# A delta-rule recurrence: whole 128x128 transposes in place of 64x64 products, one kind of work at a time

## The reference

```
def step(state, inp):
    r_t, w_t, k_t, v_t, an_t, b_t = inp
    sa = jnp.einsum('bhij,bhj->bhi', state, an_t)
    state = (state * w_t[:, :, None, :] + sa[..., None] * b_t[:, :, None, :]
             + v_t[..., None] * k_t[:, :, None, :])
    return state, jnp.einsum('bhij,bhj->bhi', state, r_t)
```

## Time and profile before

| | us |
|---|---|
| median of 3 runs | 4853.73 |
| lowest and highest | 4845.61 to 4868.58 |
| span of the profiled execution | 4860.3 |
| TensorE matmul busy in it | 4200.5 |
| VectorE, ScalarE, GpSimd busy | 2967.3, 2069.0, 1175.3 |

### The profile page before, as it was taken

The page is one execution under the profiler, slowest core; times in us unless marked ns, Lnnn a source line. Parts: engine busy times, 40 slices in busy tenths (PEclk is TensorE's granted clock), DMA queues, the critical chain, the costliest instruction groups (busy, mean ns, idle before and its releaser), DMA issues. The chain is left out here.

```text
span 4860.3 us, 142503 instructions
## 1 busy us (share of the span) xinstructions
PE 4200.5 (86%) x61166; PEld 3925.7 (81%) x61166; DVE 2967.3 (61%) x5380; ACT 2069.0 (43%) x3696; POOL 1175.3 (24%) x952
## 2 busy tenths in 40 slices
PE   6979999976999967777777769972999999999998
PEld 5869999966888857667667757762999999999998
DVE  6879999945888854444444437757444444444443
ACT  4568888844666621111111112220444444444443
POOL 4544444421444410100011113310111211112110
PEclk9989999967999988999998989985999999999999
DMA  8810000014443331122111226630655655656553
GB/s 168 185 53 23 25 25 23 24 33 146 146 143 133 124 124 56 56 59 66 56 56 56 64 73 180 200 110 28 177 170 172 181 169 178 176 175 173 175 175 104
DMA packets 519591, 542.01 MB, mean 112 GB/s; under 512 B 75200, under 2 KB 456384, under 8 KB 519104
## 3 DMA queue, kind: packets, MB, share of 16 engines
q1 hardware_dynamic: 411840, 425.00, 27.8%
q10 hardware_dynamic: 92480, 62.93, 5.5%
q0 software_dynamic: 14784, 46.57, 4.6%
HBM read 377.99 MB, written 156.43 MB: 110 GB/s over the span
## 5 line engine op out<-in xcount | busy, mean ns | idle before, releaser
L2299 DVE TENSOR_TENSOR g_wlo<-g_raw,g_whi 128x2048 fp32r<-128x2048 f32 x192 | 439.2, 2287 | 115.5 <-ACT g_whi L2261 115.5
L2261 ACT ACTIVATE g_whi<-g_raw 128x2048 fp32r<-128x2048 f32 x192 | 366.4, 1909 | 145.2 <-DMA g_raw<-expert_w_gate 145.2
L2370 PE MATMUL g_pD<-g_whi,g_hh 128*128 128x256 f32 x1536 | 417.2, 285 | 2.5 <-ACT g_o L2288 2.4
L2370 PE MATMUL g_pD<-g_wlo,g_hh 128*128 128x256 f32 x1536 | 408.1, 279 | 0.0
L1119 PE MATMUL c_pP<-c_xh,c_whi 128*128 128x258 f32 x1120 | 329.8, 294 | 35.8 <-DMA c_gup<-g_lora_up 29.5
L1271 POOL TENSOR_TENSOR d_kr<-d_kr,d_fixed 128x512 f32<-128x512 f32 x80 | 104.8, 1316 | 1007.1 <-ACT d_kr L1305 1006.9
L1384 DVE TENSOR_TENSOR d_pm<-d_pP,d_fixed 128x128 f32<-128x128 f32 x400 | 114.1, 290 | 369.9 <-PE d_pP L1441 369.3
L587 DVE TENSOR_TENSOR sapl<-sapT,saph 128x512 fp32r<-128x512 f32 x512 | 329.8, 686 | 2.7 <-ACT saph L546 2.7
L577 DVE TENSOR_REDUCE sanm<-sapS 128x1 f32<-128x1024 f32 x256 | 313.5, 1225 | 26.5 <-PE sapS L628 16.6
L1441 PE MATMUL d_pP<-d_zy,d_br 64*64 64x32 f32 x6400 | 287.3, 227 | 47.1 <-issue 46.9
L1119 PE MATMUL c_pP<-c_xh,c_wlo 128*128 128x258 f32 x1120 | 320.9, 287 | 0.0
(11 more groups left out here) (363 smaller groups left out, 14145.7 us busy)
## 6 DMA issues: line engine op xcount, KB each, us to landing
g_raw<-expert_w_gate SPq DMA_DIRECT2D x64, 1024.0 KB, 5.2
g_raw<-expert_w_up SPq DMA_DIRECT2D x64, 1024.0 KB, 8.4
g_raw<-expert_w_down SPq DMA_DIRECT2D x64, 1024.0 KB, 5.2
ops<-c_ops SPq DMA_DIRECT2D x40, 1024.0 KB, 4.2
d_bd<-ops SPq DMA_DIRECT2D x80, 512.0 KB, 3.9
c_xh<-xT_hi SPq DMA_DIRECT2D x10, 1032.0 KB, 6.1
c_xl<-xT_lo SPq DMA_DIRECT2D x10, 1032.0 KB, 8.7
x_in<-x SPq DMA_DIRECT2D x20, 512.0 KB, 7.5
```

The costliest lines, as they stand in the source:

```text
L2261: act.activation(w_hi[:, Q % NBUF, :, :], raw[:, Q % NRAW, :, :], ACT.Copy).then_inc(s["g_hi"], 1)
L2299: dve.tensor_tensor(w_lo[:, Q % NBUF, :, :], raw[:, Q % NRAW, :, :], w_hi[:, Q % NBUF, :, :].bitcast(F32), ALU.subtract).then_inc(s["g_lo" ...
L2370: mm = pe.matmul(pD[k][:, 0:WB], x[:, d, k * P:(k + 1) * P], w[:, b, d, :], start=(d == 0 and i == 0), stop=(d == DC - 1 and i == len(part ...
```

## The change

Only `recurrence` changes. Products are no longer paired by `heads`. The tiles get another order of heads: a head is (q, a, h), its results lie in partition half and column chosen so that each kind of product goes through the four quadrants in turn by itself. The transposed inverse is no longer grown: Z alone is grown, and before each level, and once after the last, it is transposed whole (two 128x128 transposes a direction), which ScalarE copies into Y. V, B and K are transposed by six 128x128 transposes. `through` and `out` no longer accumulate two kinds in one place: the parts are written to two places, ScalarE copies one and VectorE adds the other (`through`, `out` of VectorE). VectorE now makes `y_out`, and SyncE issues its stores, four for each direction and chunk. The loads are split into keys and values, and reads. Eight PSUM tiles become four of two banks' width, which brings waits between kinds that share a bank (`can_between`, `through`, `solved`, `out`, `state`). The order within a level is: transposes of both directions, `between` of both, one kind of side work of both, growth of both.

```
-        pX, pP, pZ, pS = [[ps(f"d_p{n}{g}") for g in range(2)] for n in "XPZS"]
+        pA, pB = [[ps(f"d_p{n}{g}", (P, RT, 256)) for g in range(2)] for n in "AB"]
+        left, right = [[m[:, :, k * P:(k + 1) * P] for m in pA] for k in range(2)]
+        first, second, inc = [[m[:, :, k * C:(k + 1) * C] for m in pA] for k in range(3)]
+        grow, flipped = [m[:, :, 0:C] for m in pB], [m[:, 0:2, P:2 * P] for m in pB]
...
             with sp.Fori(0, NCH // 2 - 1) as i:
                 for par in range(2):
+                    n = 2 * i + par
                     for g in range(2):
-                        sp.wait_ge(s["d_yo"], 2 * (2 * i + par) + g + 1)
+                        sp.wait_ge(s["d_bkc"], 2 * n + g + 1)
                         sp.sem_inc(s["d_seen"], 1)
-                        load(2 * i + par + 2, par, g)
+                        load_keys(n + 2, par, g)
+                    for g in range(2):
+                        sp.wait_ge(s["d_ye"], 2 * n + g + 3)
+                        sp.sem_inc(s["d_seen"], 1)
+                        load_reads(n + 2, par, g)
+                        store(n, par, g)
...
+            def join(m, par):
+                for g in range(2):
+                    stationary(m - 1, 1 - par, NL, g)
+                    keys(m, par, g)
+            def turn(n, par):
+                for l in range(NL):
+                    for g in range(2):
+                        stationary(n + 1, 1 - par, l, g)
+                    for g in range(2):
+                        if l == 0:
+                            known(n, g)
+                        if l == 1:
+                            solved(n, g)
+                        if l == 2:
+                            read(n, g)
+                        if l == 4:
+                            turned(n + 1, 1 - par, g)
...
             def begin(m, par):
                 for g in range(2):
                     dve.wait_ge(s["d_x1"], 2 * m + g + 1)
+                    dve.tensor_tensor(br[par][g][:], left[g], bc(upon[:, g:g + 1, :], [P, RT, 2 * C]), ALU.mult).then_inc(s["d_br"], 1)
+                for g in range(2):
                     dve.wait_ge(s["d_x3"], 2 * m + g + 1)
+                    dve.tensor_tensor(Z[par][g][:], grow[g], bc(beside[:, g, 0:1, :], [P, RT, C]), ALU.mult).then_inc(s["d_in"], 1)
...
+            def turn(n, par, i):
                 for l in range(NL):
                     for g in range(2):
                         between(n + 1, l, g)
+                    for g in range(2):
+                        if l == 0:
+                            through(n, g)
+                        if l == 2:
+                            out(n, par, i, g)
+                        if l == 3:
+                            state(n, par, g)
                     for g in range(2):
                         grown(n + 1, 1 - par, l, g)
...
+            def x12(m, par, g):
+                pe.wait_ge(s[f"d_la{par}{g}"], 16 * (m // 2 + 1))
+                pe.wait_ge(s[f"d_lb{par}{g}"], 32 * (m // 2 + 1))
                 if m:
                     pe.wait_ge(s["d_bkc"], 2 * (m - 1) + g + 1)
+                for q, a, h in HEADS:
+                    solve(at(left[g], a, h, q), op(par, g, OP_B, q, a, h), both(par, g, q, a, h))
+                    mm = solve(at(right[g], a, h, q), op(par, g, OP_K, q, a, h), both(par, g, q, a, h))
+                mm.then_inc(s["d_x1"], 1)
+            def x3(m, par, g):
                 if m:
+                    pe.wait_ge(s["d_Yc"], yc(m - 1, NL, g))
+                for q, a, h in HEADS:
+                    mm = solve(at(grow[g], a, h, q), op(par, g, OP_A, q, a, h), op(par, g, OP_B, q, a, h))
+                mm.then_inc(s["d_x3"], 1)
+            def turned(m, par, g):
+                pe.wait_ge(s["d_Pe"], 2 * (NL * m + NL - 1) + g + 1)
+                for k in range(2):
+                    for q in range(2):
+                        pe.transpose(left[g][:, 2 * k + q, :], bd[par][g][:, q, (OP_B, OP_K)[k], :, :].rearrange("p a t -> p (a t)"), identf[:])
+                for q in range(2):
+                    mm = pe.transpose(right[g][:, q, :], bv[par][g][:, 2 * q:2 * q + 2, :].rearrange("p a t -> p (a t)"), identf[:])
+                mm.then_inc(s["d_bk"], 1)
+            def stationary(m, par, l, g):
+                can_use(m, l, g)
+                for h in range(2):
+                    mm = pe.transpose(flipped[g][:, h, :], Z[par][g][:, 2 * h:2 * h + 2, :].rearrange("p q t -> p (q t)"), identf[:])
+                mm.then_inc(s["d_T"], 1)
+            def between(m, par, l, g, n):
+                can_between(m, l, g, n)
+                for h in range(2):
+                    for a in range(2):
+                        for q in range(2):
+                            mm = solve(packed(at(inc[g], q, a, h)[:, 0:C // 2], l), at(br[par][g], a, h, q)[:, 0:C], cols(at(Z[par][g], a, h, q), l, g))
+                mm.then_inc(s["d_P"], 1)
             def grown(m, par, l, g):
                 pe.wait_ge(s["d_Pe"], 2 * (NL * m + l) + g + 1)
+                pe.wait_ge(s["d_Yc"], yc(m, l, g))
+                for h in range(2):
+                    for q in range(2):
+                        for a in range(2):
+                            mm = solve(packed(at(grow[g], a, q, h)[:, 0:C // 2], l), at(Y[par][g], q, h, a), cols(at(pm[l][g], q, a, h), l, g))
+                mm.then_inc(s["d_Z"], 1)
...
+            def join(m, par):
                 for g in range(2):
+                    if m < NCH:
+                        x12(m, par, g)
+                    if m:
+                        stationary(m - 1, 1 - par, NL, g)
+                if m < NCH:
+                    for g in range(2):
+                        x3(m, par, g)
+            def turn(n):
+                m, par = n + 1, n % 2
+                for l in range(NL):
+                    if m < NCH:
+                        for g in range(2):
+                            stationary(m, 1 - par, l, g)
+                        for g in range(2):
+                            between(m, 1 - par, l, g, n)
+                    for g in range(2):
+                        if n >= 0:
+                            if l == 0:
+                                through(n, par, g)
+                            if l == 1:
+                                solved(n, par, g)
+                            if l == 2:
+                                out(n, par, g)
+                            if l == 3 and m < NCH:
+                                state(n, par, g)
+                        if m < NCH and l == 4:
+                            turned(m, 1 - par, g)
+                    if m < NCH:
+                        for g in range(2):
+                            grown(m, 1 - par, l, g)
```

More of the change, by code:

```diff
@@ L1315, in out @@
[L1315 to L1336 removed]
+                act.activation(tbk[par][g][:].rearrange("p k j t -> p (k j t)").rearrange("p (s c) -> p s c", c=P), left[g], ACT.Copy)
@@ L1348, in _ @@
-            turn(NCH - 1, 1, NCH // 2 - 1, False)
-            for k in ("00", "01", "10", "11"):
-                act.wait_ge(s["d_yst" + k], 16 * (NCH // 2 + 1))
+                    turn(2 * i + par, par)
+                    join(2 * i + par + 2, par)
+            turn(NCH - 2, 0)
+            for g in range(2):
+                stationary(NCH - 1, 1, NL, g)
+            for step in (known, solved, read):
+                for g in range(2):
+                    step(NCH - 1, g)
         @block.vector
@@ L1435, in _ @@
             pe.wait_ge(s["d_dm"], 16)
-            def heads(cross, out, l, r, first=True, last=True):
-                for h in range(2):
-                    mm = pe.matmul(out(halves[1 - h if cross else h]), l(halves[h]), r(halves[h]), start=first, stop=last)
-                return mm
-            def op(par, g, k, j):
-                return (lambda h: bd[par][g][h, j // 2, k, j % 2, :]) if k < OP_V else (lambda h: bv[par][g][h, j, :])
-            def both(par, g, j):
-                return lambda h: bd[par][g][h, j // 2, OP_A:OP_R + 1, j % 2, :]
@@ L1506, in can_begin, with op, both, at @@
-            def can_begin(m, par, i, g):
-                pe.wait_ge(s[f"d_ld{par}{g}"], 32 * (i + 1))
+            pe.wait_ge(s["d_id"], 2)
+            def op(par, g, k, q, a, h):
+                return bd[par][g][halves[h], q, k, a, :]
+            def both(par, g, q, a, h):
+                return bd[par][g][halves[h], q, OP_A:OP_R + 1, a, :]
+            def at(m, half, x, y):
+                return m[halves[half], 2 * x + y, :]
+            def solve(out, l, r):
+                return pe.matmul(out, l, r, start=True, stop=True)
@@ new lines, in grown, with through @@
+                mm.then_inc(s["d_Z"], 1)
+            def through(n, par, g):
+                pe.wait_ge(s["d_mask"], 2 * n + g + 1)
+                pe.wait_ge(s["d_bkc"], 2 * n + g + 1)
+                pe.wait_ge(s["d_S"], 2 * n + g + 1)
+                if n + 1 < NCH:
```

(45 more changed lines are left out.)

380 lines of the change are left out of this document (98 added, 282 removed).

## The result

| | before | after |
|---|---|---|
| median, us | 4850.53 | 4871.85 |
| lowest and highest | 4832.97 to 4874.25 | 4854.29 to 4902.17 |
| ratio, 95% interval | | 1.004 (1.0023 to 1.0057) |
| span of the profiled execution | 4860.3 | 4893.4 |

The change makes the kernel 0.4% slower, where 112 us less were forecast. Of the 33 us between the two profiled executions 29 lie between the first and the last masked product of the recurrence: 1148.5 us over 39 chunks, 29.4 us a chunk, against 28.7 by the same two marks before.

What follows compares the result with a forecast made beforehand. Delivery of TensorE's instructions was taken to bound the kernel; a chain of 24.4 plus 0.5 and 0.9 of stalls makes 25.8 against 28.6 us a chunk, 112 us saved over 40 chunks: 4742 us, range 4610 to 4880.

Steps and rivals of the forecast that it cites:

- Delivery binds the kernel before: Recurrence: TensorE stands until its next instruction packet arrives; 7.25 packets at 3.75 us plus 1.9 make 29.1 us a chunk.
- 0.5 + 0.9: Packet stalls left after the change, a chunk: 0.5 us for coincidences in the levels, 0.9 us for the burst packet.
- Instructions, loads, stores, array time at full clock: Recurrence: 708 matmul records a chunk, some 223 packets; second load covered, 7.5 against 8.9 us; array time a draw.
- The chain of hops, 22.8 us: Recurrence, a chunk: handovers between engines, five levels of 18.7 us plus a join of 4.1, at full clock.
- 0.5 for switching: Recurrence: changing between whole-array transposes and quadrants, over 20 times a chunk, taken as 0.5 us in all.
- the join's end: Between chunks: first direction's products, masks and identity addition before the first level; the whole join was priced at 4.1 us.
- 3.75, 2.7, 4.2, 4.5, 3.55 and 4.1: Chain's terms in us a chunk: levels with through, solved, out, state and turned as side work, then the join.
- "issue": TensorE's idle time in the recurrence, read as waiting for instruction packets; to fall from 250 to under 120 us.
- The clock: Recurrence: granted clock kept at the stage's 0.92, so 14 us of array work grow by 1.1 us a chunk.
- the clock falls: Rival, chance 0.05: a third more of the recurrence at slow clock, 29.4 us a chunk, about 4886; sign: under 0.85.
- the attention stage at 1.00: Argument against the clock rival: attention holds clock 1.00 though two fifths of its 5103 records are transposes.
- stalls on top of the chain: Rival, chance 0.13: late packets inside the levels add 4.8 us to 24.4, 29.2 us a chunk, 4878 us.

Runs made afterwards that it cites:

- e6: Kernel before with V and K transposed whole, 112 fewer instructions a chunk: 4827.19 us, ratio 0.9966.
- e1: Kernel before with 8 unused one-column products added ahead of each growth, 80 a chunk: 5025.68 us, ratio 1.0383.
- e15: Kernel after, with GpSimd masking a chunk's keys only once VectorE has added the identity of both directions: 4815.93 us, ratio 0.992.
- e12: Kernel after with between results in another bank, side work between transposes and between products, VectorE's growth addition ahead of side operations: 4708.02 us, ratio 0.9718.
- e5: Kernel before with one unused 256-column product added ahead of each growth, 10 a chunk: 4906.54 us, ratio 1.0112.

## Why the prediction was wrong

**Delivery binds the kernel before: right**, with the close second that e6 shows. Of the gaps over 0.25 us between TensorE's records (from one start to the next), those at packet ends were 7.6 us a chunk before and are 1.3 after, where 0.5 + 0.9 were allowed; e1 has the same period at 17% more packets. The "mostly hidden" of the Trainium skill ("Runtime: NRT & Kernel Launch", Instruction fetch mechanics) doesn't hold here.

**Instructions, loads, stores, array time at full clock: right**, as far as the runs show. 225 packets against "some 223"; no wait for a load in the list of the kernel after beyond the stage's first; TensorE's 19.4 us busy in a full-clock chunk lie in records that are spaced as those before.

**The chain of hops, 22.8 us: near, too short by about 0.9.** With the 0.5 for switching and 1.4 for packets it says 24.7 at full clock; the line says 25.6, the one chunk at full clock 25.5. The term that was off is the join's end. The timeline of TensorE gives the levels' starts in that chunk:

```profile
2546.94 0.66 PE L1539 MATMUL d_pB<-d_id,d_z 128*128 128x128 f32 x4 [0.71 <-DVE d_z L1440]
...
2549.94 0.69 PE L1539 MATMUL d_pB<-d_id,d_z 128*128 128x128 f32 x4 [0.21 <-DVE d_z L1440]
...
2554.98 0.66 PE L1539 MATMUL d_pB<-d_id,d_z 128*128 128x128 f32 x4 [0.69 <-DVE d_z L1440]
...
2559.63 0.66 PE L1539 MATMUL d_pB<-d_id,d_z 128*128 128x128 f32 x4 [1.47 <-DVE d_z L1440]
...
2563.01 1.16 PE L1502 MATMUL d_pA<-d_bd 64*64 64x128 f32 x32
```

From 2541.92 on: 5.02, 3.00, 5.04, 4.65, 3.38 and 4.40 us, against 3.75, 2.7, 4.2, 4.5, 3.55 and 4.1. The second and the last three are within 0.3. The third has a packet's stall of 0.5 in it. The first level is 1.27 longer: the tally followed only the first direction through mask and identity and let the second arrive in time. It comes 1.40 us later, 0.61 of it GpSimd's mask beside VectorE (e15), which the tally had at nothing. This chunk has only 0.6 us of "issue" stalls (0.46 and 0.17) where 1.4 are added above, so for the chain by itself the tally may be short by more, up to 1.6.

**The clock: the step that failed.** The forecast took the stage's 0.92 over from the kernel before, 1.1 us a chunk. It came out 0.78, and costs 9.2 x 0.42 = 3.9 us (0.42 is the mean of the 38 chunks), 2.8 more than allowed. 0.9 + 2.8 is the 3.7 between the forecast 25.8 and the 29.5 of these chunks. The rival "the clock falls" had this mechanism, this size (1.9 us a packet at the low level, 10.6 us a chunk, measured 9.2) and nearly this time, 4886 for 4872, and was given 0.05. Its sign came, too: a clock under 0.85. What spoke against it, the attention stage at 1.00 with two fifths of its records transposes, was a stage in which TensorE is busy 697 of 700 us; it tells nothing of one that works in pieces between hops.

The rival "stalls on top of the chain" had a time that is nearer still, 4878, by luck: its sign was that "issue" stays, and "issue" fell to 36 us. That 4872 lies inside the range of 4610 to 4880 is owed to this rival alone, for whose sake the range went so far.

So the gain didn't fail to come for want of fewer stalls: they went. TensorE still waits, 9.9 us a chunk in gaps over 0.25 us now against 9.0 before, but for its own results, and in this form the clock stays low for more than twice the share. What the half clock cost before could hide in the packets' period; now every stretch of it lies on the chain. That the clock is what was lost is shown by the same levels at both clocks, and two kernels with the same instructions (e12, e15) agree, which shorten waits and gain more than the waits; what makes it fall is only narrowed. Tiny products added raised s in both kernels (0.16 to 0.38, 0.44 to 0.66), array work ahead of the transposes lowered it, and shorter waits lowered it. Why work behind the between products lowered it by less stays open.

The splits by straight lines are approximate, since within a chunk the low level falls on other levels each time; slopes between 7 and 15 us show how much. For e5 the slope is even 28.6 (3.1), as much as the whole chunk over again: a line also takes in what goes along with a low clock.

## What to carry to other kernels

When a bound by delivery of instructions is lifted, price the chain under it at the lower clock too, and ask what the stage's share of that clock will be when its records are fewer: a clock taken over from the old stage is a guess. Then order each engine's queue so that what the next step needs comes first; here bank and order together brought 156 us to a rewrite that had cost 20. In a chain that two directions share, follow the second one as well, through the engines that run beside it.

## What the hardware showed

- An addition of VectorE with both inputs in SBUF took 1.04 us instead of 0.42 with a GpSimd operation of 1.3 us beside it, and 425 ns in all 80 cases without it. VectorE's operations that read PSUM (L1419, 0.42) weren't stretched in the same place.
- At half clock the quadrants took 32 records in 1.08 us of busy time where 0.67 do at full clock, and a level 4.18 us for 3.00.
- 24 whole transposes more in a chunk changed the kernel's time by nothing measurable, while the low level's share fell to a third.
